# Stick-breaking attention in a decoder trunk: key-block sums shared by two query blocks, and one cast moved from VectorE to ScalarE

## The chip, the cores and the metric

The kernel runs on one core of one Trainium2 chip. The metric is device time in microseconds (us) of one execution, as the median of three runs. All matrix work is float32 in value: each operand is split into a high part, rounded to the type that TensorE takes (fp32r), and a low part, the difference, so a product of two such operands takes three matmuls and a product with an exact constant takes two.

## The reference

A trunk of two layers over 512 tokens with 1024 features. The change touches the token mixer of layer 0 alone, stick-breaking attention with 16 heads of 64 features, in query blocks of 128:

```python
z = jnp.einsum("bhtd,bhsd->bhts", qb, kb).astype(jnp.float32) * scale
mask = s_idx < t_idx
log_keep = jnp.where(mask, jax.nn.log_sigmoid(-z), 0.0)
tail = lax.cumsum(log_keep, axis=3, reverse=True)
between = jnp.concatenate([tail[..., 1:], jnp.zeros_like(tail[..., :1])], axis=-1)
a = jnp.where(mask, jnp.exp(jax.nn.log_sigmoid(z) + between), 0.0)
outs.append(jnp.einsum("bhts,bhsd->bhtd", a.astype(vb.dtype), vb))
```

With softplus(z) = -log_sigmoid(-z), the weight of key s for query t is exp(z[s] minus the sum of softplus(z) over the keys from s up to t). The sum over keys is what is reorganised here.

## The kernel before

**Layout.** Keys lie on the 128 partitions and queries in the columns. For key block j (0 to 3) the PSUM bank Z[j] holds the scores of queries from block j on: 512, 384, 256 and 128 columns. `sp[j]` is softplus of it, `sph[j]` and `spl[j]` are its high and low parts. The sum over keys is added into Z[j] by matmuls: a triangle of -1 (`negtri`) times block j itself, and a square of -1 (`negones`) times each later key block, for the columns where that block has queries. The sum of blocks 2 and 3 for the last query block is already made once, on VectorE (`last_two`, the tile `both`), and its high and low parts are stored in the unused columns of `sph[2]` and `spl[2]`.

**Order.** Each engine has its own hand-written program, and the engines meet only at semaphores. Eight pairs of heads are worked through; a pair has two halves (half 0 and half 1), one head each, and the head's number is s. TensorE (function `attention_pair`) runs for one pair: `scores(p, 0)`, `values(s-1, 1)` of the head before, `transpose_v`, the Q projection of the next pair (24 matmuls), `cumulate(s)`, half of the K projection, `scores(p, 1)`, `values(s, 0)`, the rest of K and half of V, `cumulate(s+1)`, the rest of V. In the last pair the projections give way to a few blocks of the output projection. `scores` ends by raising `z_done`, `cumulate` waits for `sp_low` of each key block (key block 3 first, key block 0 last, L620) and raises `cum_done`, and `values` waits until all four low parts of the weights, `al`, are there (`a_low`, L636).

**ScalarE** in a half (its `slot`, L1690): four exponentials and four logarithms (L1698, L1703), which make softplus with VectorE's help; the copy of a finished output to `of` (L1712); in half 0 the copy of V (L1715); one weight tile's high part in half 0 and two in half 1 (`tile_high`, L1624), of which the second in half 1 waits until TensorE has begun a later tile (L1622); in half 1 `move_q` and `split_qk` for K (L1719, L1720); then four exponentials of the finished sums with the copies that make `ah` (L1726, L1729); in half 0 `split_qk` for Q; last the high part of an output (`oh`).

**VectorE** in a half (its `slot`, L1167): for each key block `softplus` (L1174), the cast to `sph` (L1180) and the subtraction to `spl` (L1030 called from L1186), with `last_two` between; then V's low part (half 0), the scaling of a projection into `att_tmp` (L1135), an output's addition (L1159), in half 1 the two low parts of K (`k_pack`, from L1145), then the four `al` (L1199), and what is left of Q, V and the outputs.

**GpSimd (POOL)** does in this stage only the low parts of the weight tiles, `wl`, as four subtractions of 256 columns for each tile, as soon as the high part is there (L504).

Nearly all copies on ScalarE carry line L1607 in the profile and all subtractions on VectorE line L1030, since helpers issue them.

Of the kernel before, what the change touches and what calls it, by code (L numbers as in the profile page):

```python
# [28 lines left out]
P = 128  # L29
# [95 lines left out]
def program(nc, xT, pT, w8, w11, params, consts, outT):  # L125
    ctx = ExitStack()
    with ctx:
        def sb(name, shape, dt=F32, where=ctx):
            return where.enter_context(nc.sbuf_tensor(name, [P] + shape, dt))
# [23 lines left out]
        with ExitStack() as ph:  # L153
            cst = sb("cst", [C_COLS - C_TRI], F32, ph)
            tmp = sb("att_tmp", [T], F32, ph)
            vf = sb("vf", [T], F32, ph)


            qh = [sb(f"qh{a}", [2, T], F32R, ph) for a in range(2)]
            q_pack = [sb(f"q_pack{a}", [2, T], F32R, ph) for a in range(2)]  # L160
            k_pack = [sb(f"k_pack{a}", [2, T], F32R, ph) for a in range(2)]

            v_pack = sb("v_pack", [2 * TB, P], F32R, ph)
            of = sb("of", [T], F32, ph)
            sp = [sb(f"sp{j}", [T - j * P], F32, ph) for j in range(TB)]
            sph = [sb(f"sph{j}", [T if j == TB - 2 else T - j * P], F32R, ph) for j in range(TB)]
            spl = [sb(f"spl{j}", [T if j == TB - 2 else T - j * P], F32R, ph) for j in range(TB)]

            both = sb("both", [P], F32, ph)
            both_h, both_l = sph[TB - 2][:, 2 * P:3 * P], spl[TB - 2][:, 2 * P:3 * P]  # L170
            ah = [sb(f"ah{j}", [T - j * P], F32R, ph) for j in range(TB)]
            al = [sb(f"al{j}", [T - j * P], F32R, ph) for j in range(TB)]
            oh, ol = sb("oh", [PAIRS, T], F32R, ph), sb("ol", [PAIRS, T], F32R, ph)
# [68 lines left out]
        z_done, z_exp, z_ln = sem("z_done"), sem("z_exp"), sem("z_ln")  # L242
        sp_full, sp_high, sp_low = sem("sp_full"), sem("sp_high"), sem("sp_low")
        both_full, both_high, both_low = (sem(n) for n in ("both_full", "both_high", "both_low"))
        cum_done, a_full, a_high, a_low = sem("cum_done"), sem("a_full"), sem("a_high"), sem("a_low")
        o_done, o_moved, o_full, o_high, o_low = (
            sem(n) for n in ("o_done", "o_moved", "o_full", "o_high", "o_low"))
# [297 lines left out]
        def _(pe):  # L545
# [71 lines left out]
            def cumulate(s):  # L617

                for jj, j in enumerate(reversed(range(TB))):
                    pe.wait_ge(sp_low, 4 * s + jj + 1)  # L620
                    if j == TB - 3:
                        pe.wait_ge(both_low, s + 1)
                    for j2 in range(j, TB if j == TB - 2 else max(j + 1, TB - 1)):
                        left = negtri if j2 == j else negones
                        out = Z[j][:, (j2 - j) * P:T - j * P]
                        parts = (sph[j2][:, 0:T - j2 * P], spl[j2][:, 0:T - j2 * P])
                        if j < j2 == TB - 2:
                            out = out.rearrange("p (a t) -> p a t", t=P)
                            parts = [part[j2][:].rearrange("p (a t) -> p a t", t=2 * P)[:, :, 0:P] for part in (sph, spl)]
                        for part in parts:  # L630
                            last = mm(out, left[:], part, start=False, stop=True, skip_group_check=True)  # L631
                    last.then_inc(cum_done, 1)
# [392 lines left out]
        def _(dve):  # L1025
# [141 lines left out]
            def slot(p, half, par_, first=False, more=True):  # L1167
                s = 2 * p + half

                def softplus(jj):  # L1170

                    j = TB - 1 - jj
                    dve.wait_ge(z_ln, 4 * s + jj + 1)
                    vec.scalar_tensor_tensor(sp[j][:], sp[j][:], SOFTPLUS_LINEAR, Z[j][:, 0:T - j * P], ALU.min, ALU.max)\  # L1174
                        .then_inc(sp_full, 1)

                def softplus_high(jj):
                    j = TB - 1 - jj
                    dve.wait_ge(sp_full, 4 * s + jj + 1)
                    vec.tensor_copy(sph[j][:, 0:T - j * P], sp[j][:]).then_inc(sp_high, 1)  # L1180

                def softplus_low(jj):
                    j = TB - 1 - jj
                    dve.wait_ge(sp_high, 4 * s + jj + 1)
                    cols = slice(0, T - j * P)
                    low(spl[j][:, cols], sp[j][:], sph[j][:, cols], sp_low)  # L1186

                def last_two():

                    vec.tensor_tensor(both[:], sp[TB - 2][:, P:2 * P], sp[TB - 1][:], ALU.add).then_inc(both_full, 1)  # L1190
                    dve.wait_ge(both_full, s + 1)
                    vec.tensor_copy(both_h, both[:]).then_inc(both_high, 1)
                    dve.wait_ge(both_high, s + 1)
                    low(both_l, both[:], both_h, both_low)

                def weights_low(jj):
                    j = TB - 1 - jj
                    dve.wait_ge(a_high, 4 * s + jj + 1)
                    low(al[j][:], sp[j][:], ah[j][:], a_low)  # L1199

                softplus(0)
                for jj in range(1, TB):
                    softplus_high(jj - 1)
                    softplus(jj)
                    softplus_low(jj - 1)
                    if jj == 2:
                        last_two()
                softplus_high(TB - 1)
                softplus_low(TB - 1)
                if half == 0:  # L1210
                    take_vt(p)
                if more:
                    take_qk(p + 1, half, 1 - par_)
                if not first:
                    take_o(s - 1, 1 - half)
                if more and half == 1:
                    take_qk_low(p + 1, 1, 1 - par_)
                for jj in range(TB):
                    weights_low(jj)
                if more and half == 0:  # L1220
                    take_qk_low(p + 1, 0, 1 - par_)
                if more and half == 1:
                    take_v(p + 1)
                if not first:
                    take_o_low(s - 1, p - (1 - half), 1 - half)
# [379 lines left out]
        def _(act):  # L1605
# [84 lines left out]
            def slot(p, half, par_, first=False, more=True, tiles=()):  # L1690
                s = 2 * p + half

                def exponential(jj):
                    j = TB - 1 - jj
                    if not first:
                        act.wait_ge(a_low, 4 * s - 4 + jj + 1)
                    act.wait_ge(z_done, 4 * s + jj + 1)
                    nc.scalar.activation(sp[j][:], Z[j][:, 0:T - j * P], ACT.Exp).then_inc(z_exp, 1)  # L1698

                def ln_one_plus(jj):  # L1700
                    j = TB - 1 - jj
                    act.wait_ge(z_exp, 4 * s + jj + 1)
                    nc.scalar.activation(sp[j][:], sp[j][:], ACT.Ln, bias=1.0).then_inc(z_ln, 1)  # L1703

                for t in range(TB + 1):
                    if t < TB:
                        exponential(t)
                    if t:
                        ln_one_plus(t - 1)
                if not first:  # L1710
                    act.wait_ge(o_done, s)
                    copy(of[head_rows(1 - half)], O[1 - half][HD:P, :], o_moved)  # L1712
                if half == 0:
                    act.wait_ge(chunk_done, 4 * p + 4)
                    copy(v_pack[:, :, 0:HD], bank[1][:].rearrange("p (g e) -> p g e", e=HD), vt_high)  # L1715
                for tile in tiles:
                    tile_high(*tile)
                if more and half == 1:
                    move_q(p + 1, 1 - par_)  # L1719
                    split_qk(p + 1, 1, 1 - par_)  # L1720
                act.wait_ge(both_full, s + 1)
                for jj in range(TB + 1):
                    j = TB - 1 - jj
                    if jj < TB:
                        act.wait_ge(cum_done, 4 * s + jj + 1)
                        nc.scalar.activation(sp[j][:], Z[j][:, 0:T - j * P], ACT.Exp).then_inc(a_full, 1)  # L1726
                    if jj:
                        act.wait_ge(a_full, 4 * s + jj)
                        copy(ah[j + 1][:], sp[j + 1][:], a_high)  # L1729
                if more and half == 0:  # L1730
                    split_qk(p + 1, 0, 1 - par_)
                if not first:
                    o_high_part(s - 1, p - (1 - half), 1 - half)
# [387 lines left out]
```

## Time and profile before

| | us |
|---|---|
| median of three runs | 1519.96 (1519.95 to 1519.98) |
| the profiled execution | 1519.65 |
| its span, first to last instruction | 1517.8 |
| TensorE busy in the span | 1494.1 (98%) |
| VectorE, ScalarE, GpSimd busy | 850.6, 676.5, 798.7 |
| the attention stage | from about 29 to 249 us of the span |

The durations below come from the one profiled execution; 1.85 us lie outside its span. TensorE's time is the kernel's time almost everywhere, so the first question to any row is whether TensorE waits there, and the second how long before TensorE's need the other engines are ready. Matmuls are pipelined, so the distance from one start to the next says what a matmul costs, and not its recorded duration. On the other engines too the next instruction may start a little before the recorded end of the one before.

### The profile page before, as it was taken

To read this page: it belongs to the slowest core of one execution; us is meant where nothing else is said; L and a number is where in the kernel's file an instruction comes from. 1 tells how busy PE (TensorE), PEld (TensorE's weight loads), DVE (VectorE), ACT (ScalarE), POOL (GpSimd) and SP (SyncE) were. 2 spreads that over 40 slices of the span, in tenths; PEclk is the share of its full clock that TensorE was granted. 3 is DMA by queue.
4 is the path that set the end of the run, shared out by engine and by line. 5 is a ranking of instruction groups with operands and counts; after the bars stand their busy time and mean duration, and the time that the engine had idled before them with its cause. 6 is when DMAs were issued, how large, how long until landed. Compare 5 with 4: busy or idle time off the path is not lost.

```text
span 1517.8 us, 19981 instructions
## 1 busy us (share of the span) xinstructions
PE 1494.1 (98%) x6806; PEld 1234.5 (81%) x6806; DVE 850.6 (56%) x1291; ACT 676.5 (45%) x1017; POOL 798.7 (53%) x984
## 2 busy tenths in 40 slices
PE   9999999999999999999999999999999999999996
PEld 6888887888888888887778888888788888888885
DVE  7999996555555411158974664646655555511145
ACT  6777885433323322247463542635633333322243
POOL 5343344666666655466255154452576666655452
PEclk9999999999999999999999999999999999999998
DMA  4111111322222422224142222321222222332221
GB/s 176 57 61 59 47 56 56 111 97 97 97 97 97 141 97 95 69 98 167 56 139 92 89 105 98 132 84 42 97 97 97 97 97 97 117 110 98 91 84 56
DMA packets 41798, 142.14 MB, mean 94 GB/s; under 512 B 4240, under 2 KB 8464, under 8 KB 41744
## 3 DMA queue, kind: packets, MB, share of 16 engines
q1 hardware_dynamic: 41168, 139.74, 26.6%
q10 hardware_dynamic: 576, 1.69, 0.3%
q8 instruction: 32, 0.52, 0.1%
q14 instruction: 22, 0.18, 0.0%
HBM read 139.32 MB, written 2.10 MB: 93 GB/s over the span
## 4 chain that ended last, share of the span: by engine, by line
PE 91%; DVE 4%; ACT 2%; POOL 1%; issue 1%; DMA 0%; DVEq 0%; SPq 0%; ACTq 0%
PE bank L553 26%; PE bank L557 26%; PE bank L556 26%; PE bank L823 3%; PE bank L827 3%; PE bank L828 3%; PE bank L631 2%; POOL wl L520 1%; DVE xl L1050 1%; PE bank L611 1%; PE bank L641 1%; PE bank L642 1%; PE bank L612 1%; ACT wh L1607 1%; DVE sumsq L1044 0%
## 5 line engine op out<-in xcount | busy, mean ns | idle before, releaser
L504 POOL TENSOR_TENSOR wl<-raw,wh 128x256 fp32r<-128x256 f32 x752 | 615.8, 850 | 478.3 <-ACT wh L1607 478.2
L553 PE MATMUL bank<-xh,wh 128*128 128x512 f32 (+1 forms) x1160 | 452.0, 390 | 3.5 <-POOL wl L520 2.2
L557 PE MATMUL bank<-xh,wl 128*128 128x512 f32 (+1 forms) x1160 | 450.2, 388 | 0.0
L556 PE MATMUL bank<-xl,wh 128*128 128x512 f32 (+1 forms) x1160 | 450.1, 388 | 0.0
L1607 ACT ACTIVATE wh<-raw 128x1024 fp32r<-128x1024 f32 (+1 forms) x212 | 235.0, 1108 | 477.9 <-PE bank L553 394.5
L553 PEld LDWEIGHTS bank<-xh,wh 128*128 128x128 f32 x1160 | 217.9, 188 | 51.4 <-DVE xl L1050 3.8
L557 PEld LDWEIGHTS bank<-xh,wl 128*128 128x128 f32 x1160 | 217.8, 188 | 44.9
L556 PEld LDWEIGHTS bank<-xl,wh 128*128 128x128 f32 x1160 | 217.9, 188 | 43.7
L520 POOL TENSOR_TENSOR wl<-raw,wh 128x256 fp32r<-128x256 f32 x160 | 128.7, 836 | 196.7 <-ACT wh L1607 196.7
L1070 DVE TENSOR_TENSOR x<-x,bank 128x512 f32<-128x512 f32 x56 | 38.5, 688 | 254.7 <-PE bank L557 254.7
L553 PE MATMUL bank<-yh,wh 128*128 128x512 f32 x352 | 136.9, 389 | 0.0
L556 PE MATMUL bank<-yl,wh 128*128 128x512 f32 x352 | 136.9, 389 | 0.0
L557 PE MATMUL bank<-yh,wl 128*128 128x512 f32 x352 | 136.9, 389 | 0.0
L1269 DVE SCALAR_TENSOR_TENSOR conv<-gate,par,conv 128x512 f32<-128x512 f32 x88 | 91.5, 1040 | 13.2 <-DVE conv L1265 5.0
L1263 DVE TENSOR_TENSOR gate<-bank,rstd 128x512 f32<-128x512 f32 x44 | 30.4, 692 | 91.8 <-PE bank L557 87.0
L553 PEld LDWEIGHTS bank<-yh,wh 128*128 128x128 f32 x352 | 66.1, 188 | 13.8
L557 PEld LDWEIGHTS bank<-yh,wl 128*128 128x128 f32 x352 | 66.1, 188 | 13.7
L556 PEld LDWEIGHTS bank<-yl,wh 128*128 128x128 f32 x352 | 66.1, 188 | 13.7
L1784 ACT ACTIVATE conv<-conv 128x512 f32<-128x512 f32 x44 | 27.9, 634 | 106.2 <-DVE conv L1269 106.2
L1272 DVE TENSOR_TENSOR up<-bank,rstd 128x512 f32<-128x512 f32 x44 | 30.4, 692 | 68.3 <-PE bank L557 68.3
L1030 DVE TENSOR_TENSOR yl<-yf,yh 128x512 f32 x44 | 41.6, 945 | 40.1 <-ACT yh L1607 40.1
L553 PE MATMUL bank<-vy,wh 128*128 128x512 f32 x128 | 50.7, 396 | 0.9 <-DVE vy L1030 0.9
(220 smaller groups left out, 2336.5 us busy)
## 6 DMA issues: line engine op xcount, KB each, us to landing
raw<-in_w SPq DMA_DIRECT2D x180, 512.0 KB, 3.2
raw<-in_w SPq DMA_DIRECT2D x32, 704.0 KB, 4.0
rc<-in_w SPq DMA_DIRECT2D x16, 512.0 KB, 4.2
w_end<-in_w SPq DMA_DIRECT2D x8, 512.0 KB, 4.4
rb<-in_w SPq DMA_DIRECT2D x8, 512.0 KB, 6.2
x<-in_xT SPq DMA_DIRECT2D x4, 512.0 KB, 6.8
outT<-x SPq DMA_DIRECT2D x8, 256.0 KB, 2.6
pin<-in_pT ACTq DMA_DIRECT2D x2, 512.0 KB, 3.1
```

The lines of the kernel that those rows point to most:

```text
L504: last = nc.gpsimd.tensor_tensor(wl[:, slot, cols], part[:, cols], wh[:, slot, cols].bitcast(F32), ALU.subtract)
L520: last = nc.gpsimd.tensor_tensor(wl[:, slot_of(n), cols], part[:, cols] if len(part.shape) == 2 else part[:, b, :], wh[:, slot_of(n), cols ...
L553: first = mm(out, ah_, bh_, start=start, stop=False, skip_group_check=True)
L556: mm(out, ah_, bl_, start=False, stop=False, skip_group_check=True)
L557: return mm(out, al_, bh_, start=False, stop=stop, skip_group_check=True)
L823: first = mm(out[:], high, wh[:, slot, cols], start=start and k == 0, stop=False, skip_group_check=True)
L827: mm(out[:], high, wl[:, slot, cols], start=False, stop=False, skip_group_check=True)
L828: last = mm(out[:], low_, wh[:, slot, cols], start=False, stop=k == KC // 2 - 1, skip_group_check=True)
L1030: vec.tensor_tensor(out, full, high.bitcast(F32), ALU.subtract).then_inc(done, 1)
L1070: vec.tensor_tensor(one(x, k), one(x, k), bank[u][:], ALU.add).then_inc(chunk_freed, 1)
L1269: vec.scalar_tensor_tensor(cv, g[:, tap:tap + T], col(par, w[tap]), cv, ALU.mult, ALU.add).then_inc(conv_step, 1)
L1607: nc.scalar.activation(out, in_, ACT.Copy, bias=0.0, scale=scale).then_inc(done, 1)
```

## The change

For key block 0, the sum over later key blocks has three parts: block 1 for the queries of blocks 1 to 3 (384 columns), block 2 for query block 2, and `both` for query block 3 (256 columns together). After the change, blocks 1 to 3 are added once on VectorE for query blocks 2 and 3 (`three_f`, 256 columns), and TensorE multiplies block 1 for query block 1 alone (128 columns) and the new sum (256 columns). Both come as high and low parts, so there are still six matmuls in the group of key block 0: 512, 512, 384, 384, 256, 256 columns before, and 512, 512, 128, 128, 256, 256 after. The tile `both` moves into spare columns of `sp[2]`, so that one strided operand reads block 2 and `both`.

VectorE gains two instructions in a half (the addition `three_f`, the subtraction `three_l`) and loses one, the 512-column cast to `sph[0]`. ScalarE gains two, behind its logarithms and ahead of the copy to `of`: the cast to `three_h`, which waits for VectorE's addition, and the cast to `sph[0]`, which waits for VectorE's softplus of key block 0.

```diff
@@ cumulate (TensorE)
+                    if j == 0:
+                        pe.wait_ge(three_low, s + 1)
+                        for out, parts in (
+                                (Z[0][:], (sph[0], spl[0])),
+                                (Z[0][:, P:2 * P], (sph[1][:, 0:P], spl[1][:, 0:P])),
+                                (Z[0][:, 2 * P:T], (three_h, three_l))):
+                            for part in parts:
+                                last = mm(out, (negtri if parts[0] is sph[0] else negones)[:], part[:], start=False,
+                                          stop=True, skip_group_check=True)
+                        last.then_inc(cum_done, 1)
+                        continue
@@ slot (VectorE)
+                def last_three():
+                    two = sp[TB - 2][:].rearrange("p (a t) -> p a t", t=2 * P)[:, :, 0:P]
+                    dve.wait_ge(sp_full, 4 * s + 3)
+                    vec.tensor_tensor(three_f[:].rearrange("p (a t) -> p a t", t=P),
+                                      sp[1][:, P:3 * P].rearrange("p (a t) -> p a t", t=P), two, ALU.add)\
+                        .then_inc(three_full, 1)
+
+                def last_three_low():
+                    dve.wait_ge(three_high, s + 1)
+                    low(three_l[:], three_f[:], three_h[:], three_low)
...
                     if jj == 2:
                         last_two()
-                softplus_high(TB - 1)
+                        last_three()
+                last_three_low()
                 softplus_low(TB - 1)
@@ slot (ScalarE)
                     if t:
                         ln_one_plus(t - 1)
+                act.wait_ge(three_full, s + 1)
+                copy(three_h[:], three_f[:], three_high)
+                act.wait_ge(sp_full, 4 * s + 4)
+                copy(sph[0][:], sp[0][:], sp_high)
                 if not first:
                     act.wait_ge(o_done, s)
```

The order on ScalarE in half 1, from the exponential of key block 0 to the first weight tile; before:

```order
L1698 ACTIVATE sp<-bank 128x512
L1703 ACTIVATE sp<-sp 128x384
L1703 ACTIVATE sp<-sp 128x512
L1607 ACTIVATE of<-bank 64x512
L1622 REGISTER_ALU
L1623 REGISTER_ALU
L1607 ACTIVATE wh<-raw 128x1024
```

and after, where L1740 belongs to the new wait:

```order
L1727 ACTIVATE sp<-bank 128x512
L1733 ACTIVATE sp<-sp 128x384
L1733 ACTIVATE sp<-sp 128x512
L1740 REGISTER_ALU
L1636 ACTIVATE three_h<-three_f 128x256
L1636 ACTIVATE sph<-sp 128x512
L1636 ACTIVATE of<-bank 64x512
L1651 REGISTER_ALU
L1652 REGISTER_ALU
L1636 ACTIVATE wh<-raw 128x1024
```

The two casts now stand ahead of everything that ScalarE does in the rest of the half. On VectorE in the same half, from the low part of `both` on; before:

```order
L1030 TENSOR_TENSOR spl<-both,sph 128x128
L1180 CAST sph<-sp 128x384
L1173 REGISTER_ALU
L1174 SCALAR_TENSOR_TENSOR sp<-sp,bank 128x512
L1030 TENSOR_TENSOR spl<-sp,sph 128x384
L1180 CAST sph<-sp 128x512
L1030 TENSOR_TENSOR spl<-sp,sph 128x512
```

and after:

```order
L1046 TENSOR_TENSOR spl<-sp,sph 128x128
L1216 TENSOR_TENSOR three_f<-sp 128x256
L1197 CAST sph<-sp 128x384
L1189 REGISTER_ALU
L1191 SCALAR_TENSOR_TENSOR sp<-sp,bank 128x512
L1046 TENSOR_TENSOR spl<-sp,sph 128x384
L1046 TENSOR_TENSOR three_l<-three_f,three_h 128x256
L1046 TENSOR_TENSOR spl<-sp,sph 128x512
```

The addition stands ahead of the last softplus, for which ScalarE's cast to `sph[0]` waits, and the 512-column cast is gone.

## Rows read from the trace of the kernel before

**Rows 1.** One stretch of steady pairs: us, busy of each engine, granted clock, DMA.
```profile
95.00:123.00 28.00, 28.00 (x153) 24.49 (x152) 25.72 (x51) 21.96 (x49) 11.11 (x12) 1.00 0.18 57
```
**Rows 2.** TensorE's waits, 20 to 260 us: us in total, times, longest.
```profile
PE bank L631 <- DVE spl L1030: 2.2, 4, 0.9
```
**Rows 3.** Timeline of TensorE, a cumulate of half 1: start, us, engine, line, what.
```profile
108.02 0.22 PE L631 MATMUL bank<-sph,negones 128*128 128x128 f32 x1
...
108.20 0.39 PE L631 MATMUL bank<-sph,negtri 128*128 128x384 f32 x1
...
108.60 0.28 PE L631 MATMUL bank<-sph,negones 128*128 128x256 f32 x1
...
109.30 0.33 PE L631 MATMUL bank<-sph,negones 128*128 128x384 f32 x1
...
109.64 0.28 PE L631 MATMUL bank<-sph,negones 128*128 128x256 f32 x1
```
**Rows 4.** TensorE: scores of half 0, values, scores of half 1, next pair's half 0.
```profile
112.65 0.22 PE L611 MATMUL bank<-qh,k_pack 128*128 128x128 f32 x1
...
114.32 0.45 PE L641 MATMUL bank<-ah,v_pack 128*128 128x512 f32 x1
...
126.61 0.22 PE L611 MATMUL bank<-qh,k_pack 128*128 128x128 f32 x1
...
140.17 0.22 PE L611 MATMUL bank<-qh,k_pack 128*128 128x128 f32 x1
```
**Rows 5.** Timeline of ScalarE in half 1 of the same pair.
```profile
99.76 0.55 ACT L1698 ACTIVATE sp<-bank 128x128 f32<-128x128 f32 x2
...
102.77 0.60 ACT L1607 ACTIVATE of<-bank 64x512 f32<-64x512 f32 x1
...
105.26 1.06 ACT L1607 ACTIVATE wh<-raw 128x1024 fp32r<-128x1024 f32 x1 [0.94 <-PE bank L553]
...
108.22 1.29 ACT L1607 ACTIVATE k_pack<-att_tmp 64x512 fp32r<-64x512 f32 x2 [0.59 <-DVE att_tmp L1135]
109.53 0.55 ACT L1726 ACTIVATE sp<-bank 128x128 f32<-128x128 f32 x2
...
111.48 1.04 ACT L1607 ACTIVATE ah<-sp 128x384 fp32r<-128x384 f32 x2
```
**Rows 6.** Timeline of VectorE in the same half 1.
```profile
102.74 0.42 DVE L1030 TENSOR_TENSOR spl<-sp,sph 128x256 fp32r<-128x256 f32 x1
...
103.86 0.35 DVE L1180 CAST sph<-sp 128x384 fp32r<-128x384 f32 x1
104.13 0.68 DVE L1174 SCALAR_TENSOR_TENSOR sp<-sp,bank 128x512 f32<-128x512 f32 x1
104.73 0.83 DVE L1030 TENSOR_TENSOR spl<-sp,sph 128x384 fp32r<-128x384 f32 x1
...
106.48 1.11 DVE L1030 TENSOR_TENSOR spl<-sp,sph 128x512 fp32r<-128x512 f32 x1
...
108.89 2.39 DVE L1030 TENSOR_TENSOR k_pack<-att_tmp,k_pack 64x512 fp32r<-64x512 f32 x2
111.31 2.13 DVE L1030 TENSOR_TENSOR al<-sp,ah 128x128 fp32r<-128x128 f32 x4
```
**Rows 7.** Timeline of POOL: its two weight tiles in that half.
```profile
104.40 7.48 POOL L504 TENSOR_TENSOR wl<-raw,wh 128x256 fp32r<-128x256 f32 x8 [9.86 <-ACT wh L1607]
```
**Rows 8.** A group by line and shape, 35 to 235 us: busy, mean ns, idle before.
```profile
L1607 ACT ACTIVATE ah<-sp 128x512 fp32r<-128x512 f32 x15 | 9.4, 625 | 0.0
```
**Rows 9.** Timeline of VectorE in half 0, before POOL starts at 118.43.
```profile
118.20 0.55 DVE L1030 TENSOR_TENSOR spl<-sp,sph 128x384 fp32r<-128x384 f32 x1
```
**Rows 10.** Timeline of ScalarE in half 0: its wait for cumulate.
```profile
121.96 0.79 ACT L1726 ACTIVATE sp<-bank 128x128 f32<-128x128 f32 x2 [3.60 <-PE bank L631]
```
**Rows 11.** Timeline of TensorE: the first head's cumulate and its two waits.
```profile
38.56 0.45 PE L631 MATMUL bank<-sph,negtri 128*128 128x384 f32 x1 [0.32 <-DVE spl L1030]
...
40.16 0.50 PE L631 MATMUL bank<-sph,negtri 128*128 128x512 f32 x1 [0.74 <-DVE spl L1030]
```

More of the change, by code:

```diff
@@ L164, in program @@
             of = sb("of", [T], F32, ph)
-            sp = [sb(f"sp{j}", [T - j * P], F32, ph) for j in range(TB)]
+            sp = [sb(f"sp{j}", [T if j == TB - 2 else T - j * P], F32, ph) for j in range(TB)]
             sph = [sb(f"sph{j}", [T if j == TB - 2 else T - j * P], F32R, ph) for j in range(TB)]
             spl = [sb(f"spl{j}", [T if j == TB - 2 else T - j * P], F32R, ph) for j in range(TB)]
-            both = sb("both", [P], F32, ph)
+            both = sp[TB - 2][:, 2 * P:3 * P]
             both_h, both_l = sph[TB - 2][:, 2 * P:3 * P], spl[TB - 2][:, 2 * P:3 * P]
+            three_f = sb("three_f", [2 * P], F32, ph)
+            three_h, three_l = sb("three_h", [2 * P], F32R, ph), sb("three_l", [2 * P], F32R, ph)
             ah = [sb(f"ah{j}", [T - j * P], F32R, ph) for j in range(TB)]
@@ L244, in program @@
         both_full, both_high, both_low = (sem(n) for n in ("both_full", "both_high", "both_low"))
+        three_full, three_high, three_low = (sem(n) for n in ("three_full", "three_high", "three_low"))
         cum_done, a_full, a_high, a_low = sem("cum_done"), sem("a_full"), sem("a_high"), sem("a_low")
@@ L1173, in softplus @@
                     dve.wait_ge(z_ln, 4 * s + jj + 1)
-                    vec.scalar_tensor_tensor(sp[j][:], sp[j][:], SOFTPLUS_LINEAR, Z[j][:, 0:T - j * P], ALU.min, ALU.max)\
+                    part = sp[j][:, 0:T - j * P]
+                    vec.scalar_tensor_tensor(part, part, SOFTPLUS_LINEAR, Z[j][:, 0:T - j * P], ALU.min, ALU.max)\
                         .then_inc(sp_full, 1)
@@ L1179, in softplus_high @@
                     dve.wait_ge(sp_full, 4 * s + jj + 1)
-                    vec.tensor_copy(sph[j][:, 0:T - j * P], sp[j][:]).then_inc(sp_high, 1)
+                    vec.tensor_copy(sph[j][:, 0:T - j * P], sp[j][:, 0:T - j * P]).then_inc(sp_high, 1)
                 def softplus_low(jj):
@@ L1185, in softplus_low @@
                     cols = slice(0, T - j * P)
-                    low(spl[j][:, cols], sp[j][:], sph[j][:, cols], sp_low)
+                    low(spl[j][:, cols], sp[j][:, cols], sph[j][:, cols], sp_low)
                 def last_two():
-                    vec.tensor_tensor(both[:], sp[TB - 2][:, P:2 * P], sp[TB - 1][:], ALU.add).then_inc(both_full, 1)
+                    vec.tensor_tensor(both, sp[TB - 2][:, P:2 * P], sp[TB - 1][:], ALU.add).then_inc(both_full, 1)
                     dve.wait_ge(both_full, s + 1)
-                    vec.tensor_copy(both_h, both[:]).then_inc(both_high, 1)
+                    vec.tensor_copy(both_h, both).then_inc(both_high, 1)
                     dve.wait_ge(both_high, s + 1)
-                    low(both_l, both[:], both_h, both_low)
+                    low(both_l, both, both_h, both_low)
+                def last_three():
[7 more added lines that the diff above has]
+                    low(three_l[:], three_f[:], three_h[:], three_low)
                 def weights_low(jj):
@@ L1198, in weights_low @@
                     dve.wait_ge(a_high, 4 * s + jj + 1)
-                    low(al[j][:], sp[j][:], ah[j][:], a_low)
+                    low(al[j][:], sp[j][:, 0:T - j * P], ah[j][:], a_low)
                 softplus(0)
@@ L1697, in exponential @@
                     act.wait_ge(z_done, 4 * s + jj + 1)
-                    nc.scalar.activation(sp[j][:], Z[j][:, 0:T - j * P], ACT.Exp).then_inc(z_exp, 1)
+                    nc.scalar.activation(sp[j][:, 0:T - j * P], Z[j][:, 0:T - j * P], ACT.Exp).then_inc(z_exp, 1)
                 def ln_one_plus(jj):
@@ L1702, in ln_one_plus @@
                     act.wait_ge(z_exp, 4 * s + jj + 1)
-                    nc.scalar.activation(sp[j][:], sp[j][:], ACT.Ln, bias=1.0).then_inc(z_ln, 1)
+                    part = sp[j][:, 0:T - j * P]
+                    nc.scalar.activation(part, part, ACT.Ln, bias=1.0).then_inc(z_ln, 1)
                 for t in range(TB + 1):
@@ L1725, in slot @@
                         act.wait_ge(cum_done, 4 * s + jj + 1)
-                        nc.scalar.activation(sp[j][:], Z[j][:, 0:T - j * P], ACT.Exp).then_inc(a_full, 1)
+                        nc.scalar.activation(sp[j][:, 0:T - j * P], Z[j][:, 0:T - j * P], ACT.Exp).then_inc(a_full, 1)
                     if jj:
                         act.wait_ge(a_full, 4 * s + jj)
-                        copy(ah[j + 1][:], sp[j + 1][:], a_high)
+                        copy(ah[j + 1][:], sp[j + 1][:, 0:T - (j + 1) * P], a_high)
                 if more and half == 0:
```

## The prediction

> **What bounds the kernel now.** I read the stretch table first: in 28 us of steady pairs TensorE is busy for 28.00, at a granted clock of 1.00, which is its level of 2.4 GHz; VectorE is busy for 25.72 and ScalarE for 21.96 [rows 1]. So columns taken from TensorE are worth their time there, but only as long as nobody makes TensorE wait, and VectorE has little room. Then TensorE's waits: in the whole attention stage it waits for the softplus parts 4 times, 2.2 us in all [rows 2], at the two ends of the stage and never in a steady pair. One steady pair takes 140.17 - 112.65 = 27.52 us [rows 4]. The rest is a question of slack, and for that I laid the timelines of the engines in one half 1 side by side [rows 4 to 7].
>
> **TensorE: what is saved.** Two matmuls of 384 columns become two of 128. By starts, the pair of 384 columns costs 109.64 - 109.30 = 0.34 us, a pair of 128 costs 108.20 - 108.02 = 0.18, so 0.16 is saved. Behind a pair of 128, the next pair of 384 costs 0.40 instead of 0.34 [rows 3], so the least saving is 0.10; the most is 512 columns at 2.4 GHz, 0.21. I take 0.16, as it comes from the same shapes. For 16 heads that is 2.6 us (1.6 to 3.4), if TensorE never waits.
>
> **The sums themselves.** VectorE's addition of 256 columns occupies it for about 0.33 us, the distance from a 256-column subtraction to the instruction after it (0.42 recorded) [rows 6]. It is placed ahead of the cast that starts at 103.86, so the last softplus starts at 104.46 instead of 104.13 and ends at 105.14 [rows 6]. The removed cast of 512 columns stood behind it. The last part, `spl[0]`, then comes at: 384-column subtraction from 105.06 (0.55 if POOL is idle, [rows 9]), `three_l` about 105.5 to 105.9, `spl[0]` to about 106.6, where before it ended at 106.48 + 1.11 = 107.59 [rows 6]. TensorE needs it after 108. The new sum costs TensorE nothing here, in either half; the cover is the 24 matmuls of a projection ahead of `cumulate`.
>
> **ScalarE: what is pushed back.** This is the term that I think decides. Before, ScalarE goes from its last logarithm straight to the copy to `of` at 102.77 [rows 5]. After, it must wait for the softplus of key block 0, to 105.14, and then cast 512 columns, 0.63 recorded and about 0.52 to the next start [rows 8]; the cast to `three_h` fits into that wait. The copy to `of` starts at about 105.7, 2.9 us later. Behind it stand two weight tiles, the moves of Q, the split of K, the four exponentials and the `ah` copies. The gaps there give 0.94 + 0.59 us back [rows 5], so the first exponential of the weights comes at about 110.87 instead of 109.53 and the last `ah` ends at 113.86 instead of 112.52: 1.35 us late. In half 0 the same insertion meets an idle time of 3.60 us [rows 10], which takes most of it.
>
> **VectorE and POOL: what that does to `al`.** TensorE's `values` of the head waits for all four `al`. Before, they end at 111.31 + 2.13 = 113.44 [rows 6], and TensorE starts `values` at 114.32 [rows 4]: slack 0.88 us. After, K's high parts come 1.35 us late, so the two K subtractions (2.39 us together) run from 110.24 to 112.65. The weight tiles on ScalarE stand right behind the copy to `of` and are pushed by the same 2.9 us, and with them POOL's 7.48 us of subtractions: they start at about 107.3 instead of 104.40 [rows 7] and end near 114.8 instead of 111.9. That matters because a VectorE subtraction with both inputs in SBUF is slower while POOL works: 384 columns take 0.83 us with POOL active and 0.55 without [rows 6, 9], 512 columns 1.11 [rows 6]. Before, only the first `al` ran beside POOL; after, the second and third do as well, and I charge each with the 0.3 us by which the 384-column subtractions differ. So the last `al` ends at 112.65 + 2.13 + 0.6 = 115.4. The lower end is an `al` chain that POOL never slows: the last `ah` at 113.86 and one 512-column subtraction behind it give about 114.6. The upper end adds for the fourth `al` the 0.5 us between 1.11 and what it takes with POOL idle: 115.9.
>
> The Trainium skill ("SBUF — State Buffer", section "Who interferes with whom") says that a VectorE instruction with two SBUF inputs and a GpSimd instruction that reads SBUF exclude each other for a whole instruction. The rows show a smaller price than a whole POOL instruction; what the rule would give is rival D below.
>
> **The ring.** The wait feeds itself. ScalarE's first exponential (99.76) leads to `al` at 115.4, 15.65 us later; TensorE goes from `values` to the next `scores(p, 1)` in 126.61 - 114.32 = 12.29 us [rows 4], less 0.16; about 0.5 us later the first scores are finished and ScalarE's next half 1 starts. 15.65 + 12.13 + 0.5 is 28.3 us, and VectorE, which now enters half 1 later than ScalarE, adds about 0.1. So a pair takes about 28.4 us instead of 27.52, 0.85 more, and TensorE stands in front of `values` for about 1.2 us in each pair. In half 0 ScalarE starts its weights some 1.4 us later than before, while TensorE is 1 us later too, so nothing is late there.
>
> **The sum.** Seven times TensorE meets `values` of a half 1 in a following pair. The first ring starts with a credit: in the first head TensorE's two waits, 0.32 and 0.74 us [rows 11], go, since POOL's tile is pushed out of VectorE's way. That makes 7 x 0.85 - 1.06 = +4.9 us. In the last pair there are no projections to cover anything, and its own waits (the rest of the 2.2 us of [rows 2]) move about; I put it at +0.2 with its saving taken in. Behind the attention the two kernels are the same. From the profiled execution, 1519.65 (span 1517.8), this gives 1524.75; the median stands 0.3 above that execution, so **1525.0 us**.
>
> **Rivals.**
> A, the forecast: ScalarE's order and POOL's overlap make `al` late in every pair, +5 us. For it: slack 0.88 against a push of 1.35 that follows from ScalarE's program alone. Against it: each step is an extrapolation of tenths.
> B, the overlap with POOL costs nothing new: `al` at 114.6, a ring of 14.84 + 12.13 + 0.5 = 27.5 us, so a pair takes what it took, and only the first head's 1.06 and some 0.4 of savings at the ends are left: 1518.5 us, no difference. It would hold if the `al` fall between POOL's instructions. From 114.7 on it turns into A.
> C, the saving arrives whole: -2.6 - 1.06 = 1516.3 us (1515.5 with 0.21 for a head), faster. It needs `al` before 114.1, so a push of ScalarE's under 0.7 us, for instance if the softplus for which it waits comes half a us earlier. Against it: that softplus is the last of an unbroken chain on VectorE.
> D, slower still: VectorE and POOL shut each other out for whole instructions. POOL's 8 take 0.94 us each [rows 7]. Each K subtraction would take that and its own 0.7, so both end at 113.5; the first two `al` then wait for one POOL instruction each, and the last ends at about 117.1. The ring is 17.3 + 12.1 + 0.5 = 29.9 us, and 7 x 2.4 - 1.06 is +16: 1536 us. Against it: the two K subtractions take 1.2 us each in POOL's presence [rows 6, 7], not 1.6. The cited rule stands beside this rival.
> That the change doesn't do what it says gets nothing: the order of the instructions shows its columns and places.
>
> **The numbers.** Chances: A 0.60, B 0.24, C 0.10, D 0.03, and 0.03 for something between A and D. A measurement of this kernel tells 0.2%, 3.0 us, from no change. A's own range is 1521.5 to 1529.5 (`al` at 114.9 to 115.9 in the ring), of which about 0.06 lies under 1523, and B gives 0.01 to faster. So slower is 0.54 + 0.03 + 0.03 = 0.60, same 0.06 + 0.23 = 0.29, faster 0.11. The range that leaves no more than 2 in 10 out takes in A and B: 1517.5 to 1529.5.
>
> **What would show it.** In the profile after: (1) TensorE's waits name the `values` matmul (`ah`, `v_pack`) or its weight load, released by VectorE's `al`, some 7 times, 1 to 1.5 us each. (2) A steady pair by starts of `scores` takes 28.2 to 28.6 us. (3) In half 1 the copy to `of` starts 2.9 us after the last logarithm. (4) POOL's 7.5 us piece starts 3 us later in the pair and covers most `al`, whose recorded durations rise. (5) The first head's `cumulate` has no wait. (6) The group of key block 0 takes 0.16 us less. The forecast is wrong if (1) is missing: then either ScalarE's push is smaller than 0.7 us, or VectorE catches up. It is wrong in size if the pair's time lies far from 28.4, and the step to look at is then POOL's price on the `al`.

## The result, and the profile after

The changed kernel takes 1527.42 us (median of 5 runs, 1527.07 to 1527.44) against 1519.95 for the kernel before in the same comparison: a ratio of 1.005, 95% interval 1.0039 to 1.0062, 7.5 us slower. The forecast was 1525.0, slower, with a chance of 0.60, and its range of 1517.5 to 1529.5 took in no difference as well.

TensorE's waits in the attention stage of the kernel after (us in total, times, longest; L657 is the matmul of `values` with `ah`):

```profile
PE bank L657 <- DVE al L1046: 8.9, 8, 1.4
PE bank L647 <- DVE spl L1046: 1.2, 1, 1.2
```

The stretch that answers to [rows 1] (us; busy time of TensorE, its weight loads, VectorE, ScalarE and POOL; granted clock; DMA):

```profile
95.00:123.00 28.00, 26.83 (x147) 23.20 (x146) 24.60 (x52) 22.51 (x50) 9.65 (x12) 1.00 0.17 57
```

TensorE, at the same granted clock of 1.00, stands still for 1.17 us. VectorE is less busy than before (24.60 against 25.72) and POOL too (9.65 against 11.11); only ScalarE is busier (22.51 against 21.96), and it is far from full. The time went into waiting.

ScalarE in half 1, the answer to [rows 5]:

```profile
100.98 0.55 ACT L1727 ACTIVATE sp<-bank 128x128 f32<-128x128 f32 x2
...
105.54 0.42 ACT L1636 ACTIVATE three_h<-three_f 128x256 fp32r<-128x256 f32 x1 [1.56 <-DVE three_f L1216]
106.41 0.63 ACT L1636 ACTIVATE sph<-sp 128x512 fp32r<-128x512 f32 x1 [0.45 <-DVE sp L1191]
107.07 0.60 ACT L1636 ACTIVATE of<-bank 64x512 f32<-64x512 f32 x1
107.57 1.99 ACT L1636 ACTIVATE wh<-raw 128x1024 fp32r<-128x1024 f32 x2
...
110.89 1.29 ACT L1636 ACTIVATE k_pack<-att_tmp 64x512 fp32r<-64x512 f32 x2
112.20 0.55 ACT L1760 ACTIVATE sp<-bank 128x128 f32<-128x128 f32 x2
```

Counted from the first exponential, the copy to `of` starts at 6.09 us instead of 3.01, K's parts at 9.91 instead of 8.46, the weights at 11.22 instead of 9.77. The gaps of 0.94 and 0.59 us are used up. VectorE and POOL in that half, the answers to [rows 6] and [rows 7]:

```profile
111.56 2.36 DVE L1046 TENSOR_TENSOR k_pack<-att_tmp,k_pack 64x512 fp32r<-64x512 f32 x2 [2.59 <-ACT k_pack L1636]
113.95 2.67 DVE L1046 TENSOR_TENSOR al<-sp,ah 128x128 fp32r<-128x128 f32 x4
```

```profile
108.69 6.58 POOL L509 TENSOR_TENSOR wl<-raw,wh 128x256 fp32r<-128x256 f32 x8 [9.58 <-ACT wh L1636]
```

VectorE stands idle for 2.59 us until ScalarE gives it K's high part, and then makes the four `al`, the first two of them beside POOL, which works until 115.27: 2.67 us instead of 2.13. Singly, the `al` of 256 columns takes 0.96 us where it took 0.41 before; the other three take what they took (about 0.72, 0.55 and 0.68). The last ends at 116.62, and 0.13 later TensorE goes on.

### The profile page after: what moved, and what is told of

The parts are those of the page before. It is cut to its first block, busy times and chain, and to the rows that moved or that the text cites. A ratio compares the mean times of both kernels' runs of the same rounds, so it can differ in the third digit from the quotient of the medians.

```text
span 1525.6 us, 20045 instructions
## 1 busy us (share of the span) xinstructions
PE 1492.3 (98%) x6806; PEld 1231.8 (81%) x6806; DVE 846.2 (55%) x1307; ACT 689.2 (45%) x1049; POOL 787.7 (52%) x984
## 4 chain that ended last, share of the span: by engine, by line
PE 86%; DVE 7%; ACT 4%; issue 2%; POOL 1%; DMA 0%; SPq 0%; DVEq 0%; ACTq 0%
PE bank L558 25%; PE bank L562 25%; PE bank L561 25%; PE bank L839 3%; PE bank L844 3%; PE bank L843 3%; POOL wl L525 1%; DVE al L1046 1%; ACT wh L1636 1%; DVE xl L1066 1%; DVE k_pack L1046 1%; PE bank L647 1%; PE bank L657 1%; ACT q_pack L1636 1%; PE bank L658 1%
## 5 line engine op out<-in xcount | busy, mean ns | idle before, releaser
L509 POOL TENSOR_TENSOR wl<-raw,wh 128x256 fp32r<-128x256 f32 x752 | 604.9, 837 | 497.1 <-ACT wh L1636 497.1
L525 POOL TENSOR_TENSOR wl<-raw,wh 128x256 fp32r<-128x256 f32 x160 | 128.7, 836 | 196.8 <-ACT wh L1636 196.8
```

What stands on the lines that cost most here:

```text
L509: last = nc.gpsimd.tensor_tensor(wl[:, slot, cols], part[:, cols], wh[:, slot, cols].bitcast(F32), ALU.subtract)
L525: last = nc.gpsimd.tensor_tensor(wl[:, slot_of(n), cols], part[:, cols] if len(part.shape) == 2 else part[:, b, :], wh[:, slot_of(n), cols ...
```

## The ring in numbers

TensorE in the kernel after, from one `scores(p, 1)` to the next (compare [rows 4]):

```profile
100.31 0.22 PE L616 MATMUL bank<-qh,k_pack 128*128 128x128 f32 x1
...
113.74 0.22 PE L616 MATMUL bank<-qh,k_pack 128*128 128x128 f32 x1
...
115.35 0.22 PE L619 MATMUL bank<-maskneg,ident_r 128*128 128x128 f32 x1
116.75 0.49 PE L657 MATMUL bank<-ah,v_pack 128*128 128x512 f32 x1 [1.17 <-DVE al L1046]
...
126.11 0.28 PE L635 MATMUL bank<-three_l,negones 128*128 128x256 f32 x1
...
129.00 0.22 PE L616 MATMUL bank<-qh,k_pack 128*128 128x128 f32 x1
...
129.16 0.27 PE L619 MATMUL bank<-maskneg,ident_r 128*128 128x128 f32 x1
```

and ScalarE at the end of half 0 in the same pair:

```profile
126.43 0.60 ACT L1760 ACTIVATE sp<-bank 128x512 f32<-128x512 f32 x1
126.92 1.03 ACT L1636 ACTIVATE ah<-sp 128x384 fp32r<-128x384 f32 x2
127.86 1.27 ACT L1636 ACTIVATE qh<-att_tmp 64x512 fp32r<-64x512 f32 x2
129.04 0.61 ACT L1636 ACTIVATE oh<-of 64x512 f32 x1
129.67 0.55 ACT L1727 ACTIVATE sp<-bank 128x128 f32<-128x128 f32 x2
```

A pair takes 129.00 - 100.31 = 28.69 us, 1.17 more than the 27.52 before. The pieces: ScalarE's first exponential to the last `al`, 100.98 to 116.62, is 15.64; to `values`, 0.13; TensorE from `values` to the end of half 0's `cumulate`, 116.75 to 126.39, is 9.64; 0.04 to ScalarE's exponential of key block 0; from there to its next half 1, 3.24. Together 28.69. So the ring leaves TensorE at the end of half 0's `cumulate`, not at the next `scores`: when ScalarE starts half 1 at 129.67, the scores for which it needs to wait, those of key block 3 (129.16 + 0.27 = 129.43), have already been there for 0.24 us.

## Experiments

Each kernel is timed against the kernel before on the same chip (medians of 1519.66 to 1519.76 us there). Where an experiment starts from the kernel after, it is compared with its 1527.4 us, which come from the comparison at the top; the kernel before reads 1519.95 there, so such differences are good to about 0.3 us. The diffs leave out declarations, and the comments in them are added here.

### TensorE's saving alone

```diff
+                        if j == 0 and j2 == 1:
+                            out, parts = out[:, 0:P], [part[:, 0:P] for part in parts]
                         for part in parts:
```

> The kernel before, with the two 384-column matmuls of key block 0 cut to their first 128 columns and nothing put in their place: block 1's sum is left out for query blocks 2 and 3. This is the saving on TensorE by itself. The group of key block 0 went from 1.05 to 0.92 us in the kernel after, 0.13 for a head, so if nobody makes TensorE wait: 16 x 0.13 = 2.1 us less, about 1517.8 us. If TensorE's columns are no price at all here (other engines set the pair's time), no change, 1519.9 us.

Measured: 1517.72 us against 1519.76, ratio 0.9986 (0.9977 to 0.9995), 2.0 us less. TensorE bounds a steady pair before the change, and fewer columns are worth what they take. In the kernel after, the group of key block 0 reads:

```profile
125.31 0.40 PE L635 MATMUL bank<-sph,negtri 128*128 128x512 f32 x1
...
125.77 0.22 PE L635 MATMUL bank<-sph,negones 128*128 128x128 f32 x1
...
125.94 0.33 PE L635 MATMUL bank<-three_h,negones 128*128 128x256 f32 x1
...
126.23 0.40 PE L558 MATMUL bank<-xh,wh 128*128 128x512 f32 x1
```

The pair of 128 columns takes 0.17 us, but the pair of 256 behind it 0.29 instead of the 0.24 of [rows 3]: 0.92 us for the group, 0.13 less.

### One part alone: the cast on ScalarE

```diff
-                softplus_high(TB - 1)          # VectorE
+                act.wait_ge(sp_full, 4 * s + 4)   # ScalarE, behind the logarithms
+                copy(sph[0][:], sp[0][:], sp_high)
```

> The kernel before with one part of the change alone: the cast to sph[0] is on ScalarE, behind the logarithms and ahead of the copy to `of`. Theory P (the place of the casts on ScalarE, which must wait there for VectorE's last softplus, is the cost): ScalarE goes on at about 105.4 instead of 105.7 in the pair looked at, so most of the loss is there, 1522 to 1524.5 us. Theory V (the new sum ahead of VectorE's last softplus is the cost): no sum here, so the time is that of the kernel before, 1519.5 to 1520.5 us.

Measured: 1525.36 us, ratio 1.0036 (1.0023 to 1.0049), +5.6 us. TensorE's `scores(p, 1)` and ScalarE's cast:

```profile
99.70 0.22 PE L611 MATMUL bank<-qh,k_pack 128*128 128x128 f32 x1
...
128.15 0.22 PE L611 MATMUL bank<-qh,k_pack 128*128 128x128 f32 x1
```

```profile
105.47 0.63 ACT L1606 ACTIVATE sph<-sp 128x512 fp32r<-128x512 f32 x1 [2.09 <-DVE sp L1174]
```

A pair takes 28.45 us. Theory P is borne out: 0.93 of the 1.17 us come with the cast alone, and the time is above the upper end of what I had expected. The remaining 0.24 come with the new sum, which stands ahead of the softplus for which ScalarE waits. ScalarE's first exponential to the last `al` takes 15.30 us here and 15.64 in the kernel after, 0.34 more, about what the addition occupies; less the 0.13 saved on TensorE's way that leaves 0.21 of the 0.24.

### The wait without the work, and the work without the wait

```diff
+                act.wait_ge(sp_full, 4 * s + 4)   # ScalarE, behind the logarithms; no cast
```

> The kernel before, in which ScalarE waits at the place of the casts for VectorE's last softplus and casts nothing (the cast stays on VectorE): the wait without the work. ScalarE goes on 2.1 us later in half 1, 0.5 to 0.6 of it behind the gaps, and POOL moves 2.1 us later, which makes the al some 0.4 to 0.6 us longer; with a slack of 0.88 the pair becomes 0.1 to 0.4 us longer and the first head wins its 1 us or so: 1519.5 to 1522 us. If wait and work cost only together, as the slack says, neither alone comes near cast_only's +5.6 us.

```diff
+                copy(spare[:, T:], rstd[:, 0:2 * P], spare_done)   # same place, no wait for VectorE
+                copy(spare[:, 0:T], rstd[:], spare_done)
```

> The kernel before, with two more copies on ScalarE at the place of the two casts, 256 and 512 columns of a tile that is long there, into a spare tile that nobody reads: the work of the casts without their wait. It is 0.9 us for a half. If the wait for VectorE is what costs: in half 1 the gaps of 0.94 and 0.59 us take it, in half 0 the 3.6 us do, so no change, 1519.0 to 1520.5 us. If it is ScalarE's extra work: 1524 us and more.

Measured: the wait alone 1520.31 us, ratio 1.0004 (0.9995 to 1.0013); the work alone 1519.30, ratio 0.9998 (0.9989 to 1.0007). Neither can be told from no change in time. The pair tells them apart. With the wait alone:

```profile
98.33 0.22 PE L611 MATMUL bank<-qh,k_pack 128*128 128x128 f32 x1
...
126.12 0.22 PE L611 MATMUL bank<-qh,k_pack 128*128 128x128 f32 x1
```

That is 27.79 us, 0.27 more. Over seven pairs it makes 1.9 us, of which the first head gives 1.4 back (its second `scores` starts at 42.62 instead of 44.05), so little is seen in the whole time. With the work alone a pair keeps 27.52. Both came as expected. The costs don't add, because the slack takes the first microseconds: work 0.9 us, free; wait 2.1 us, 0.27; the wait and the 512-column cast together, 0.93.

### Both casts on VectorE

```diff
-                act.wait_ge(three_full, s + 1)
-                copy(three_h[:], three_f[:], three_high)
-                act.wait_ge(sp_full, 4 * s + 4)
-                copy(sph[0][:], sp[0][:], sp_high)
...
+                dve.wait_ge(three_full, s + 1)
+                vec.tensor_copy(three_h[:], three_f[:]).then_inc(three_high, 1)
+                softplus_high(TB - 1)
                 last_three_low()
```

ScalarE's wait for `both_full` ahead of its weights becomes one for `three_full`, since the sum reads what the weights overwrite and the cast that waited for it is gone from ScalarE.

> The kernel after with both casts (three_h and sph[0]) on VectorE, nothing new on ScalarE. Theory P: ScalarE is not held back, TensorE's wait in front of values goes from 1.2 us to under 0.5; VectorE has some 1.0 to 1.5 us more in each half and comes near its limit, so 1518 to 1522 us. Theory V: VectorE's chain is what delays, it is longer still, so as slow as the kernel after or slower, 1527 us and above.

Measured: 1532.43 us, ratio 1.0086 (1.0071 to 1.0102), slower still. By the time this is what theory V says, and my expectation under P was 10 us off; the profile shows another mechanism. VectorE in half 1, and ScalarE:

```profile
108.80 0.83 DVE L1238 CAST three_h<-three_f 128x256 fp32r<-128x256 f32 x1
109.56 0.95 DVE L1197 CAST sph<-sp 128x512 fp32r<-128x512 f32 x1
110.44 0.96 DVE L1046 TENSOR_TENSOR three_l<-three_f,three_h 128x256 fp32r<-128x256 f32 x1
111.32 1.22 DVE L1046 TENSOR_TENSOR spl<-sp,sph 128x512 fp32r<-128x512 f32 x1
```

```profile
113.17 1.28 ACT L1639 ACTIVATE k_pack<-att_tmp 64x512 fp32r<-64x512 f32 x2 [2.29 <-DVE att_tmp L1151]
```

ScalarE is on time with its tiles again, so POOL works beside just these four instructions: the 256-column subtraction takes 0.96 us where it takes 0.42 alone [rows 6]. `spl[0]` and `att_tmp` are late, TensorE waits in `cumulate` (7.3 us in 16 times), and ScalarE waits 2.29 us for `att_tmp` before it can split K. VectorE is busy for 26.96 of 28 us. A steady pair takes about 28.75 us, hardly more than the 28.69 of the kernel after; that the time is longer still lies at the two ends of the stage. The profiled execution, the fastest of four, has a span 3.4 us longer than that of the kernel after: 1.7 of it in the first head, where TensorE's waits are back, and 1.4 in the last pair, with a wait of 1.6 us. So VectorE has no room for the new sum with both casts. The kernel after was right to take a cast away from VectorE and wrong in where it put it; VectorE with one of the two casts was not tried.

### The same casts, later on ScalarE

```diff
-                act.wait_ge(three_full, s + 1)
-                copy(three_h[:], three_f[:], three_high)
-                act.wait_ge(sp_full, 4 * s + 4)
-                copy(sph[0][:], sp[0][:], sp_high)
                 if not first:
                     ...
                 if half == 0:
                     ...
+                if tiles:
+                    tile_high(*tiles[0])
+                act.wait_ge(three_full, s + 1)
+                copy(three_h[:], three_f[:], three_high)
+                act.wait_ge(sp_full, 4 * s + 4)
+                copy(sph[0][:], sp[0][:], sp_high)
-                for tile in tiles:
+                for tile in tiles[1:]:
                     tile_high(*tile)
```

> The kernel after with its two casts moved on ScalarE behind the copy to `of`, the copy of V and the first weight tile, so that they start when VectorE has the sums ready; no work is added or taken away. Theory P: ScalarE is pushed by half a microsecond at most, which its old gap of 0.59 us takes, TensorE's wait in front of values goes, and the columns' saving of 2.1 us and the first head's wait are left: 1517 to 1518.5 us. Theory V: no change against the kernel after, 1527 us.

Measured: 1518.38 us, ratio 0.9991 (0.9982 to 1.0). ScalarE in half 1:

```profile
102.40 0.60 ACT L1636 ACTIVATE of<-bank 64x512 f32<-64x512 f32 x1
102.90 1.05 ACT L1636 ACTIVATE wh<-raw 128x1024 fp32r<-128x1024 f32 x1
103.94 0.42 ACT L1636 ACTIVATE three_h<-three_f 128x256 fp32r<-128x256 f32 x1
104.80 0.64 ACT L1636 ACTIVATE sph<-sp 128x512 fp32r<-128x512 f32 x1 [0.45 <-DVE sp L1191]
```

The wait of 1.56 us is gone because ScalarE does other work meanwhile; what stays is 0.45, in the place of the old gap of 0.94. Nothing is added or taken away against the kernel after, and 9.0 us are won. Against the kernel before, the 1.4 us are hardly clear of no difference. That rules theory V out: VectorE's addition still stands ahead of its last softplus.

### One half at a time

The casts are moved as above in half 0 alone, or in half 1 alone.

> The kernel after, with the two casts moved behind the first weight tile in half 0 alone; half 1 stays as it is. Theory F (my forecast's ring: half 1 delays TensorE, TensorE delays ScalarE's next half, and in half 0 nothing is late): half 0's order is no part of it, so no change, 1527 us. Theory G (the ring is ScalarE and VectorE through both halves, TensorE only follows): in half 0 the softplus for which ScalarE waits is itself late by half 1's push, and without that wait ahead of its tile ScalarE reaches its weights earlier, so TensorE's events take over and the pair falls from 28.7 to about 28.4 us: 1525 to 1526.5 us.

> The kernel after, with the two casts moved behind the first weight tile in half 1 alone; half 0 stays as it is. Both theories: half 1 no longer pushes K's parts and the last al, VectorE enters half 0 in time, and half 0's idle time of 3.6 us on ScalarE takes the casts: within 0.5 us of the kernel with both moved (1518.4 us). If half 0's place mattered by itself it would be 1520 us or more.

Measured: half 0 alone 1529.16 us, ratio 1.0062 (1.0046 to 1.0077); half 1 alone 1516.85 us, ratio 0.9981 (0.9972 to 0.999), the fastest of all. TensorE's `scores(p, 1)` with half 0 moved, and ScalarE there:

```profile
101.63 0.22 PE L616 MATMUL bank<-qh,k_pack 128*128 128x128 f32 x1
...
130.32 0.22 PE L616 MATMUL bank<-qh,k_pack 128*128 128x128 f32 x1
```

```profile
125.80 0.79 ACT L1767 ACTIVATE sp<-bank 128x128 f32<-128x128 f32 x2 [1.47 <-PE bank L647]
```

Again 28.69 us: although ScalarE is ready 1.47 us early, the pair is no shorter, for `cumulate` in half 0 comes when TensorE comes. Theory G, a ring without TensorE, falls. Theory F had the pair right, but the whole is 1.7 us slower than the kernel after instead of equal to it. That lies at the ends: the first head's wait (1.22 us) is back and its second `scores` starts at 44.10 instead of 42.77, and the last pair loses the rest. TensorE with half 1 moved:

```profile
97.33 0.22 PE L616 MATMUL bank<-qh,k_pack 128*128 128x128 f32 x1
...
124.59 0.22 PE L616 MATMUL bank<-qh,k_pack 128*128 128x128 f32 x1
```

A pair takes 27.26 us, as with both moved. As a whole it is 1.5 us faster, where I had expected them within 0.5. The difference lies almost wholly in the first head, and half 0's place matters there alone. There the casts ahead of the tile keep POOL away from VectorE's softplus chain (POOL's second tile starts at 39.7, and at 35.8 with both moved), and TensorE's two waits [rows 11] are gone (its second `scores` starts at 42.77 in the kernel after, at 44.05 before); with the casts behind the tile TensorE waits 1.21 us there again.

### TensorE's columns in the kernel after

```diff
-                                (Z[0][:, P:2 * P], (sph[1][:, 0:P], spl[1][:, 0:P])),
+                                (Z[0][:, P:T], (sph[1][:], spl[1][:])),
```

> The kernel after, with the two 128-column matmuls of key block 0 made 384 columns wide again, so TensorE does as much as in the kernel before (block 1 is counted twice for query blocks 2 and 3). Theory F (ring through TensorE): 0.13 us of them lie in the ring, 0.13 x 7 = 0.9 us more, and with the ends some 1.2 us: 1528.6 us. Theory G (ring without TensorE): the columns come out of TensorE's wait of 1.2 us for each pair, so under 0.4 us, all of it at the stage's ends: 1527.4 to 1527.8 us.

Measured: 1528.35 us, ratio 1.0057 (1.0043 to 1.007), 0.9 more than the kernel after; against the kernel before on the same chip it is 8.7 us, where the kernel after has 7.5. A pair takes 28.80 us, 0.11 more. If TensorE only followed, its 1.17 us of waiting would swallow the columns; instead one group of them lies in the ring. That is theory F, a ring through TensorE, and the 1.2 us between 8.7 and 7.5 are what it expected.

### POOL out of the way

```diff
-                for b in range(0, blocks, LOW_BLOCKS):
+                for b in range(0, LOW_BLOCKS if light else blocks, LOW_BLOCKS):
```

> The kernel after, in which POOL makes one of its four subtractions for a weight tile of the attention stage from the fourth tile on (the other three quarters of wl keep old values), so that it is out of VectorE's way early. If POOL's overlap costs the al and K subtractions what the durations say (K 1.18 instead of 0.69 us each, al 2.67 instead of about 1.9 us for four), the last al comes 0.7 us earlier, the limit set by ScalarE's last ah, and the pair falls by about as much: 1522 to 1524 us. If the overlap costs nothing on the path, 1527 us.

> Control for pool_light_after: the kernel before with POOL's subtractions in the attention stage cut to one in four from the fourth tile on. TensorE waits for nobody in a steady pair here, so a faster VectorE is worth nothing there: 1519 to 1520.5 us; at most some tenths at the stage's last pair. If it falls by 4 us like the other, then POOL's share in this stage is a price by itself and pool_light_after says nothing about the change.

Measured: with the kernel after 1522.97 us, ratio 1.0022 (1.0012 to 1.0031), 4.5 less than with POOL's full work. With the kernel before 1518.18, ratio 0.999 (0.9981 to 0.9999), 1.5 less, and its steady pair keeps 27.52 us. I had expected at most some tenths, at the last pair; the 1.5 us are all in the first head, whose waits of [rows 11] are gone (the second `scores` starts at 42.59 instead of 44.05). That shows POOL as the cause of those waits. The kernel after has lost them already, so they are no part of its 4.5 us. VectorE with the kernel after and little work on POOL:

```profile
109.99 1.41 DVE L1048 TENSOR_TENSOR k_pack<-att_tmp,k_pack 64x512 fp32r<-64x512 f32 x2 [2.59 <-ACT k_pack L1638]
111.56 0.29 DVE L1048 TENSOR_TENSOR al<-sp,ah 128x128 fp32r<-128x128 f32 x1 [0.16 <-ACT ah L1638]
112.24 0.43 DVE L1048 TENSOR_TENSOR al<-sp,ah 128x256 fp32r<-128x256 f32 x1 [0.39 <-ACT ah L1638]
113.14 1.21 DVE L1048 TENSOR_TENSOR al<-sp,ah 128x384 fp32r<-128x384 f32 x2 [0.47 <-ACT ah L1638]
```

K's parts take 1.41 us instead of 2.36, and VectorE now waits for ScalarE's `ah`. The last `al` ends 14.93 us after ScalarE's first exponential (99.42), close to the 14.84 of the prediction's lower bound. TensorE's `scores(p, 1)` there:

```profile
98.74 0.22 PE L618 MATMUL bank<-qh,k_pack 128*128 128x128 f32 x1
...
126.70 0.22 PE L618 MATMUL bank<-qh,k_pack 128*128 128x128 f32 x1
```

A pair takes 27.96 us, 0.73 less. So of the 1.17 us of loss in a pair, 0.73 need POOL beside VectorE and 0.44 do not. (TensorE saves 0.26 us in a pair, as the kernel before with TensorE's saving alone shows by a pair of 27.26 us, so measured from there the loss is 1.43, and 0.70 of it do not need POOL.)

## Why the prediction was right, and where it was off

**Direction and mechanism: right.** ScalarE's casts wait for VectorE, what stands behind them is pushed past the slack of `al`, and POOL's displaced work lengthens the K and `al` subtractions. The cast alone on ScalarE, the casts later on ScalarE, and POOL out of the way each show one of these steps.

**Step by step.** (1) TensorE waits before `values` with 8.9 us in 8 waits: as said, the eighth in the last pair. (2) A pair takes 28.69 us; I had said 28.2 to 28.6. (3) The copy to `of` starts 3.08 us later, said 2.9. (4) POOL's piece starts at 7.71 us behind the first exponential instead of 4.64, 3.07 later, and the `al` take 2.67, said 2.73; but the piece takes 6.58 us, not 7.5, and covers two `al`, not most of them. (5) The first head's waits are gone. (6) The group is 0.13 shorter, said 0.16. From the first exponential to the last `al` the trace has 15.64 us, the prediction 15.65. That close an agreement is partly luck: I charged the second and the third `al` with 0.3 us each, while the second alone pays 0.55 and the third, which starts when POOL has ended, pays nothing.

**The size: one term too small.** The forecast was +5.1 us, the result +7.5. The mis-sized term is the ring's way back. I let it end with "about 0.5 us later the first scores are finished and ScalarE's next half 1 starts", 12.13 + 0.5 + 0.1 us from `values`, and wrote of half 0 that nothing is late there. It measures 0.13 + 9.64 + 0.04 + 3.24 = 13.05: ScalarE waits for half 0's `cumulate` and then has its last weights, Q's parts and an output ahead of half 1. That is 0.3 us in each of seven pairs, 2.2 us. The rows to see it in were there: before the change ScalarE's half 1 starts at 99.76 [rows 5], while [rows 4] put the scores one period earlier, at 126.61 - 27.52 = 99.09. The difference of 0.67 is longer than the scores take, so ScalarE was not waiting for them. ScalarE's own way from the exponential of key block 0 to its next half 1 stands in the trace of before too, with the same 3.24 us (127.28 - 124.04):

```profile
124.04 0.60 ACT L1726 ACTIVATE sp<-bank 128x512 f32<-128x512 f32 x1 [0.24 <-PE bank L631]
...
127.28 0.55 ACT L1698 ACTIVATE sp<-bank 128x128 f32<-128x128 f32 x2
```

**The ends.** The first head gave back 1.28 us, its saved columns included, said 1.06. From the last `scores` of the stage on, 0.9 us are lost where I had put 0.2. Together with seven pairs of 1.17 that is 8.2 - 1.3 + 0.9 = 7.8, the difference of the spans. One slip in the sum: by the prediction's own terms an `al` at 115.9 gives 1528.5 us, not the 1529.5 that it has as A's upper end; the result lies below both.

**Rivals.** B (the overlap costs nothing) falls: with most of POOL's work gone a pair takes 27.96, and with all of it 28.69. C had the full saving of TensorE; it is there (TensorE's saving alone), but needs the casts elsewhere. D (VectorE and POOL shut each other out for whole instructions) would have given a pair of 29.9 us. The Trainium skill ("SBUF — State Buffer", section "Who interferes with whom") says that a VectorE instruction with two SBUF inputs contends with a GpSimd instruction that reads SBUF, and that the port pair they share is an exclusive lock. Here POOL's eight instructions take 0.82 us each in the kernel after, and a K subtraction beside them 1.18 against 0.70 alone: 0.48 more on average, the direction of the rule and rather more than half of its price. Nor do the two take turns throughout: POOL's shortest subtraction takes 0.73 us, eight of them 5.8, and the two K and two `al` subtractions beside them 2.1 alone; one after another that is 7.9 us, while all of it was done in the 6.9 from 108.69 to 115.55.

## What to carry to other kernels

An instruction moved to another engine brings its wait along, and everything behind it on that engine's queue is pushed by it, for nothing while there is slack and in full once the slack is used; put it behind work that is ready, so that its input is there when its turn comes. Here the same change costs 7.5 us with its casts in one place and wins 2.8 with half 1's in another. When slack is used up and a ring closes, follow it once around through every engine and ask at each station which of two events came last, since the period is the sum of those. And a pushed tile on one engine moves a third engine's work: look at what it will then run beside.

## What the runs showed of the hardware

A VectorE cast is hurt by POOL as much as a subtraction is: with both casts on VectorE the 256-column cast takes 0.83 us beside POOL, where the larger one of 384 columns in [rows 6] takes 0.35 alone; the subtraction of 256 columns goes from 0.42 to 0.96. And TensorE's wait as the trace lists it (1.17 us) is less than what the wait costs. From the first matmul of `scores` to the first of `values` TensorE takes 116.75 - 113.74 = 3.01 us in the kernel after and 114.32 - 112.65 = 1.67 before [rows 4], 1.34 more. The row counts from the recorded end of the matmul before (115.35 + 0.22), and where nothing is waited for the next matmul starts ahead of that end.
